# Gated branch of a layer kernel: gate units placed one by one between the chunk steps

## The reference, cut to what matters

```python
log_a = jax.nn.log_sigmoid((g_l @ w2 + g_bias)) / GLA_GATE_NORM
cum = jnp.cumsum(log_a.reshape(b, nc, CHUNK, GLA_HEADS, GLA_DK), axis=2)   # CHUNK = 64, nc = 4
q_dec, k_inv, k_to_end = q * jnp.exp(cum), k * jnp.exp(-cum), k * jnp.exp(cum_last - cum)
attn = jnp.where(tril, jnp.einsum('bnihd,bnjhd->bnhij', q_dec, k_inv), 0.0)
o_intra = jnp.einsum('bnhij,bnjhv->bnihv', attn, v)
def step(state, inp):
    q_c, k_c, v_c, d_c = inp
    o_c = jnp.einsum('bihd,bhdv->bihv', q_c, state)
    return state * d_c[..., None] + jnp.einsum('bjhd,bjhv->bhdv', k_c, v_c), o_c
o = rms_norm(o_intra + o_inter) * norm_g
o_gla = (o * silu(z)) @ w_o                       # z: "gz"
merged = sigmoid(gate_a) * o_mla + sigmoid(gate_b) * o_rwkv + sigmoid(gate_c) * o_gla   # gate_c: "gc"
```

## Time and profile before

| | us |
|---|---|
| median of 3 runs | 2073.42 |
| lowest, highest | 2066.02, 2075.84 |
| span of the profiled execution | 2070.8 |
| TensorE busy | 1960.2 |
| VectorE busy | 1314.5 |
| ScalarE busy | 704.8 |
| GpSimd busy | 77.0 |

### The profile page before, as it was taken

One profiled execution on the slowest core, in us unless ns is written; L12 is line 12 of the kernel. 1 busy time (PEld: TensorE's weight loads), 2 busy tenths in 40 slices (PEclk: granted clock), 3 DMA queues, 4 the chain that ended last, 5 costly groups with the idle time before them and its releaser, 6 DMA issues.

```text
span 2070.8 us, 41540 instructions
## 1 busy us (share of the span) xinstructions
PE 1960.2 (95%) x18039; PEld 1806.4 (87%) x18039; DVE 1314.5 (63%) x1710; ACT 704.8 (34%) x1011; POOL 77.0 (4%) x123
## 2 busy tenths in 40 slices
PE   8998999999799999999998999898999998999898
PEld 8887999998599999989877889897988887889887
DVE  8895388747647866854765358566764576339555
ACT  5562233434623332130423132233231334122233
POOL 2000000000400000020000000000001000000000
PEclk9999999999999999999999999999999999999989
DMA  8544377853437794636430246354654540235433
GB/s 220 141 126 153 120 249 258 269 139 112 121 120 258 241 260 101 171 95 170 115 93 14 76 115 179 82 153 113 174 143 115 140 123 4 63 103 172 113 107 108
DMA packets 473063, 291.41 MB, mean 141 GB/s; under 512 B 26679, under 2 KB 467484, under 8 KB 472776
## 3 DMA queue, kind: packets, MB, share of 16 engines
q1 hardware_dynamic: 466688, 262.20, 45.1%
q0 software_dynamic: 5312, 25.32, 3.2%
q10 hardware_dynamic: 904, 1.58, 0.3%
HBM read 288.02 MB, written 1.05 MB: 140 GB/s over the span
## 4 chain that ended last, share of the span: by engine, by line
PE 82%; DVE 12%; ACT 3%; issue 2%; DMA 1%; POOL 0%; DVEq 0%; ACTq 0%; SPq 0%
PE bank L702 40%; PE bank L1412 6%; PE bank L1414 6%; PE bank L1413 6%; PE bank L691 4%; PE bank L661 2%; PE bank L891 2%; DVE rounded L727 2%; PE bank L883 2%; PE bank L784 1%; PE bank L1599 1%; PE bank L1612 1%; PE bank L1057 1%; PE bank L1580 1%; PE bank L1464 1%
## 5 line engine op out<-in xcount | busy, mean ns | idle before, releaser
L702 PE MATMUL bank<-rounded 128*128 128x256 f32 (+1 forms) x4440 | 540.7, 283 | 10.0 <-DVE rounded L727 7.5
L702 PEld LDWEIGHTS bank<-rounded 128*128 128x128 f32 (+1 forms) x4440 | 531.0, 189 | 16.5 <-DVE rounded L727 10.1
L727 DVE TENSOR_TENSOR rounded<-arena,rounded 128x1024 fp32r<-128x1024 f32 (+1 forms) x243 | 293.2, 1213 | 87.2 <-ACT rounded L716 69.1
L1412 PE MATMUL bank<-parts 128*128 128x256 f32 x1024 | 290.5, 284 | 2.4 <-DVE parts L2164 2.4
L1413 PE MATMUL bank<-parts 128*128 128x256 f32 x1024 | 289.8, 283 | 0.0
L1414 PE MATMUL bank<-parts 128*128 128x256 f32 x1024 | 289.7, 283 | 0.0
L702 PE MATMUL bank<-common,arena 128*128 128x256 f32 x1280 | 285.2, 380 | 0.0
L702 PEld LDWEIGHTS bank<-common,arena 128*128 128x128 f32 x1280 | 240.1, 189 | 39.6 <-issue 4.8
L767 ACT ACTIVATE arena<-bank 128x512 f32<-128x512 f32 x114 | 67.8, 598 | 440.5 <-PE bank L702 427.9
L1412 PEld LDWEIGHTS bank<-parts 128*128 128x128 f32 x1024 | 196.5, 192 | 3.2 <-DVE parts L2164 2.1
L1413 PEld LDWEIGHTS bank<-parts 128*128 128x128 f32 x1024 | 196.5, 192 | 0.1
(11 more groups left out here) (389 smaller groups left out, 2509.3 us busy)
## 6 DMA issues: line engine op xcount, KB each, us to landing
arena<-in_w_in SPq DMA_DIRECT2D x190, 512.0 KB, 3.8
whole<-in_ffn_w_gate_up SPq DMA_DIRECT2D x44, 1024.0 KB, 5.2
arena<-in_ada_w POOLq DMA_DIRECT2D x32, 768.0 KB, 6.5
whole<-in_ffn_w_down SPq DMA_DIRECT2D x16, 1408.0 KB, 7.2
arena<-in_rec_w_in SPq DMA_DIRECT2D x36, 512.0 KB, 3.8
arena<-in_att_w_qkv SPq DMA_DIRECT2D x24, 512.0 KB, 3.7
arena<-in_rec_w_out SPq DMA_DIRECT2D x16, 512.0 KB, 3.5
arena<-in_mla_w_o SPq DMA_DIRECT2D x16, 512.0 KB, 3.7
```

The source lines that it names most:

```text
L702: last = pe.matmul(psum[s][0:c, m % 2 * T:m % 2 * T + T], w[a][:, k, cols], x[b][:, k, :], start=(k, a, b) == (0, 0, 0), stop=k == job.kt ...
L727: dve.tensor_tensor(raw_view(job_of[u], u, UNIT_LOW), raw, high_view(job_of[u], u).bitcast(F32), ALU.subtract)\
L1412: pe.matmul(bank, w_hi, x_hi, start=start and k == 0, stop=False)
```

## The change

The loop over tiles in `gla_pe` is taken apart into five functions, and the calls are put in a new order:

| TensorE, before | TensorE, after |
|---|---|
| gv, gz 0 to 7 | gv, gz 0 to 3 |
| turn 0, scores 0 | turn 0, scores 0, scores 1 |
| chunk states 0, 1 | gz 4, state 0, turn 1, gz 5, state 1 |
| heads of tile 0 | gz 6, heads of tile 0 |
| turn 1, scores 1, state 2 | state 2, gz 7 |
| heads of tile 1 | heads of tile 1 |
| sums, gc 0 to 7, go | gc 0, gc 1, sums, gc 2 to 7, go |

VectorE and ScalarE follow this order. VectorE now makes the low part of gz 7 behind both scores, that of gc 0 ahead of state 1, that of gc 1 ahead of state 2, and that of gc 2 behind the squares. ScalarE takes gz 0 to 3, copies the keys of both tiles, takes gz 4 and 5, makes the high parts of gc 0 and 1, takes gz 6 and 7, and only then loads the table of logarithms. The keys and scores of the second tile have buffers of their own, which lie on GY and GC.

```diff
--- before
+++ after
         G2 = buf(512)
-        KTT = [buf(4, P) for _ in range(2)]
-        AT = buf(4, P)
+        KTT = [[buf(4, P) for _ in range(2)], [flat(GY)[:, c * 512:c * 512 + 512].rearrange("p (a b) -> p a b", a=4) for c in range(2)]]
+        AT = [buf(4, P), flat(GC)[:, 0:512].rearrange("p (a b) -> p a b", a=4)]
         GS = [None] + [buf(4, T) for _ in range(3)]
...
@@ -1797,28 +1797,32 @@
 
         def gla_pe(j):
             pe.wait_ge(layer_split.sem, layer_split.due(pe))
-            for n in ("gv", "gz"):
-                multiply_units(j[n])
+            multiply_units(j["gv"])
+            multiply_units(j["gz"], range(4))
             pe.wait_ge(taken[0].sem, halves(0, j["gv"]))
             pe.wait_ge(taken[1].sem, halves(1, j["gv"]))
             pe.wait_ge(gla_operands.sem, gla_operands.due(pe))
-            for t in range(TT):
+
+            def turn_keys(t):
+                turn_pe([KTE[:, h, t * P:t * P + P] for h in range(4)], abanks)
+
...
+
+            def chunk_state(t, c):
+                for h in range(0, 4, 2):
+                    bank, free, done = vbanks.fill()
+                    pe.wait_ge(free.sem, free.due(pe))
+                    for n in range(2):
+                        last = pe.matmul(bank[:, n * T:n * T + T], KTT[t][c][:, h + n, :], GV[:, t, (h + n) * T:(h + n) * T + T], start=True, stop=True)
+                    last.then_inc(done, 1)
...
                         hh, v = h + n // 2, n % 2
                         o = bank[:, n * P:n * P + P]
-                        last = pe.matmul(o, GV[:, t, hh * T + v * P:hh * T + v * P + P], AT[:, hh, :], start=True, stop=False)
+                        last = pe.matmul(o, GV[:, t, hh * T + v * P:hh * T + v * P + P], AT[t][:, hh, :], start=True, stop=False)
                         for c in range(2):
                             g = 2 * t + c
                             if g:
...
                     last.then_inc(done, 1)
+
+            turn_keys(0)
+            inner_scores(0)
+            inner_scores(1)
+            multiply_units(j["gz"], range(4, 5))
+            pe.wait_ge(token_major.sem, token_major.due(pe))
+            chunk_state(0, 0)
+            turn_keys(1)
+            multiply_units(j["gz"], range(5, 6))
+            chunk_state(0, 1)
+            multiply_units(j["gz"], range(6, 7))
+            heads_of_tile(0)
+            pe.wait_ge(token_major.sem, token_major.due(pe))
+            chunk_state(1, 0)
+            multiply_units(j["gz"], range(7, 8))
+            heads_of_tile(1)
+            multiply_units(j["gc"], range(2))
             sums_pe(SQG, 2, 4)
-            multiply_units(j["gc"])
+            multiply_units(j["gc"], range(2, 8))
             multiply_units(j["go"], pieces=(branch_ready, 1))
 
         @block.tensor
...
             dve.tensor_tensor(KTE, GK, GD, ALU.mult)\
                .then_inc(gla_operands.sem, 1)
             dve.wait_ge(gla_operands.sem, gla_operands.due(dve))
-            split_v(j["gz"].through())
+            split_v(j["gz"].first + 6)
...
+            inner_scores(0)
+            inner_scores(1)
+            split_v(j["gz"].through())
+            next_state(0)
+            split_v(j["gc"].first)
+            next_state(1)
+            dve.nop().then_inc(gla_states.sem, 1)
+            heads_of_tile(0)
+            split_v(j["gc"].first + 1)
+            next_state(2)
+            dve.nop().then_inc(gla_states.sem, 1)
+            heads_of_tile(1)
             squares_v(OG, SQG, DK)
+            split_v(j["gc"].first + 2)
             dve.wait_ge(taken[0].sem, halves(0, j["gz"]))
             dve.wait_ge(taken[1].sem, halves(1, j["gz"]))
             dve.tensor_tensor(OG, OG, GZ, ALU.mult)\
@@ -3412,17 +3442,20 @@
             act.wait_ge(gla_exps.sem, gla_exps.due(act))
             high_act(j["ro"].through())
             take_units(act, j["gv"], keep_tokens(GV))
-            take_units(act, j["gz"], keep(GZ, ACT.Silu))
-            logarithms_act()
+            take_units(act, j["gz"], keep(GZ, ACT.Silu), only=range(2))
             for t in range(TT):
                 bank, full, free = abanks.empty()
                 act.wait_ge(full.sem, full.due(act))
                 for c in range(2):
                     sig = free if c else scalar_step
-                    act.activation(flat(KTT[c]), bank, ACT.Copy, scale=half[:, c:c + 1])\
+                    act.activation(flat(KTT[t][c]), bank, ACT.Copy, scale=half[:, c:c + 1])\
                        .then_inc(sig.sem, 1)
                     act.wait_ge(sig.sem, sig.due(act))
                 act.nop().then_inc(token_major.sem, 1)
+            take_units(act, j["gz"], keep(GZ, ACT.Silu), only=range(2, 3))
+            high_act(j["gc"].first + 1)
+            take_units(act, j["gz"], keep(GZ, ACT.Silu), only=range(3, 4))
+            logarithms_act()
             high_act(j["gc"].first + 2)
             rms_act(256, 4)
             take_units(act, j["gc"], keep(GT, ACT.Sigmoid), high_before(j["gc"], 2))
```

More of the change, by code:

```diff
@@ L1804, in gla_pe, with inner_scores @@
             pe.wait_ge(gla_operands.sem, gla_operands.due(pe))
-            for t in range(TT):
+            def turn_keys(t):
+                turn_pe([KTE[:, h, t * P:t * P + P] for h in range(4)], abanks)
+            def inner_scores(t):
                 here = slice(t * P, t * P + P)
-                turn_pe([KTE[:, h, here] for h in range(4)], abanks)
                 bank, free, done = vbanks.fill()
@@ L1812, in gla_pe, with heads_of_tile @@
                 last.then_inc(done, 1)
[L1813 to L1821, removed]
+            def chunk_state(t, c):
[5 more added lines that the diff above has]
+                    last.then_inc(done, 1)
+            def heads_of_tile(t):
                 pe.wait_ge(gla_states.sem, gla_states.due(pe))
@@ L2872, in gla_v, with inner_scores @@
             dve.wait_ge(gla_operands.sem, gla_operands.due(dve))
-            split_v(j["gz"].through())
+            split_v(j["gz"].first + 6)
             dve.wait_ge(taken[0].sem, halves(0, j["gv"]))
             dve.wait_ge(taken[1].sem, halves(1, j["gv"]))
-            for t in range(TT):
-                here = slice(t * P, t * P + P)
+            def inner_scores(t):
                 bank, full, free = vbanks.empty()
                 dve.wait_ge(full.sem, full.due(dve))
-                dve.tensor_tensor(AT, bank.rearrange("p (a b) -> p a b", a=4), over(const("upto"), 4,
-                    P), ALU.mult)\
+                dve.tensor_tensor(AT[t], bank.rearrange("p (a b) -> p a b", a=4), over(const("upto"), 4, P), ALU.mult)\
@@ L2882, in gla_v @@
                    .then_inc(free.sem, 1)
                 dve.wait_ge(free.sem, free.due(dve))
[L2884 to L2903, removed]
@@ L2904, in gla_v, with next_state @@
-                dve.nop().then_inc(gla_states.sem, 1)
-                if t == TT - 1:
-                    split_v(j["gc"].first + 1)
+            def next_state(g):
+                for h in range(0, 4, 2):
+                    bank, full, free = vbanks.empty()
+                    dve.wait_ge(full.sem, full.due(dve))
+                    for n in range(2):
+                        b = bank[:, n * T:n * T + T]
+                        sig = free if n else vector_step
+                        if g == 0:
+                            dve.tensor_copy(GS[1][:, h + n, :], b)\
+                               .then_inc(sig.sem, 1)
+                        else:
+                            dve.scalar_tensor_tensor(GS[g + 1][:, h + n, :], GS[g][:, h + n, :],
+                                EL[:, (h + n) * 4 + g:(h + n) * 4 + g + 1], b, ALU.mult, ALU.add)\
+                               .then_inc(sig.sem, 1)
+                        dve.wait_ge(sig.sem, sig.due(dve))
@@ L2907, in gla_v, with heads_of_tile @@
+            def heads_of_tile(t):
+                here = slice(t * P, t * P + P)
                 for h in range(0, 4, 2):
```

## The result

| | before | after |
|---|---|---|
| median of 6 runs, us | 2073.48 | 2055.52 |
| lowest to highest, us | 2066.02 to 2080.30 | 2052.68 to 2060.13 |
| span of the profiled execution, us | 2070.8 | 2053.9 |

The ratio of after to before is 0.9913, interval 0.9894 to 0.9931: the changed kernel is 18.0 us, or 0.9%, faster. Two later measurements of the same pair gave 0.9901 (0.9874 to 0.9927) and 0.9891 (0.9861 to 0.992). The forecast was 2057.0 in 2050 to 2068.5. The run of the profiled execution took 2055.73 us, so 1.8 us lie around its span.

A forecast was written before the change was run, and what follows sets the result against it. The prediction took the order of TensorE's queue as the bound. Waits gave 10.8 us and the clock 5.6, together 16.4 off 2073.4: 2057.0 us, range 2050 to 2068.5.

The forecast's parts named there:

- Work that stays: TensorE's pure small steps in one layer's gated branch, start to start without waits: 20.39 us, nothing added or dropped.
- The wait that stays: Before the heads of tile 0, TensorE still waits 0.4 us of 1.50, as gc0's low part precedes state 1.
- Waits that go: Waits for keys (2.12, 0.65 us), state 2 and squares in the gated branch were to be covered or removed.
- The new wait: Inside gc, before its fourth unit, TensorE waits 1.58 us; gc's later end gives back 2.54 us a layer.
- S+4.46: Start of gc's fourth unit, 4.46 us behind S, the end of the sums; it was wanted at S+2.88.
- The 3.30 us wait: Behind gc, TensorE stands 3.30 us until the output weights' first low parts are made; forecast to stay.
- Sum of the waits: Gated branch and gc: waits of 8.18 + 0.17 us become 0.4 + 2.54, gaining 5.4 a layer, 10.8 in both.
- Clock: Second layer's branch lost 7.31 us to low clock; 5.6 us expected back, with 0 and 7.3 as ends.
- (1): Only the waits count; the new order doesn't alter the clock's losses: 2062.6 us, chance 0.22.
- (2): The clock loss moves into gc, where new waits come, 5.7 us back: 2068.3 us, chance 0.16.
- (3): Slower: the small steps spread among units run at 1.2 GHz in both layers: 2096 us, chance 0.04.
- (4): ScalarE high part, VectorE low part, state chain paces TensorE; waits move and don't shrink: 2070 us, chance 0.08.

The follow-up runs named there:

- experiment 4: Changed kernel with one unit of gc ahead of the sums, and VectorE's low parts of gc0 and the first two output units moved: 2038.27 us, ratio 0.9839.
- Experiment 2: Changed kernel with the four gate units put ahead of all chunk steps again, the rest kept: 2081.44 us, ratio 1.0039 to the kernel before.
- Experiments 1 and 3: 1: kernel before with its five waits a branch filled, 2068.78 us; 3: changed kernel with no or one gc unit ahead of the sums, 2054.56 and 2050.16 us.
- filled kernel: Kernel before, own order, with filler matmuls in front of the five waits of each gated branch: 2068.78, 2067.55 and 2068.10 us in three timings.

## Why the prediction was right

- **Work that stays, 20.39 us a layer.** Right. From the first turn to the heads of tile 0 the sum gives 15.24 us with the wait of 0.4 in it; it is 1315.18 - 1299.94 = 15.24. From the first turn to the end of the sums it gives 20.39 + 6 x 2.88 + 0.39 = 38.06; it is 37.88. Switching between steps and units costs nothing in sum.
- **The wait that stays, 0.4 us.** Its cause was right: it is released by VectorE's states behind the low part of gc0, and in experiment 4 it went when that low part was moved. Behind the end of unit 5 (1310.06) the heads start at +5.12, forecast +5.05. That the row's 0.37 equals the forecast is in part luck: the forecast counts from start to start, and counted so, unit 6 and the wait take 1315.18 - 1311.59 = 3.59 us, 0.71 more than the 2.88 of a unit, while state 1 ahead of them took 1.53 where 1.78 was put. In experiment 4 the move was worth 0.64 us.
- **Waits that go.** None stands before states, scores, second heads or sums. Experiment 2 shows that the units between the steps cover the waits for the states: without them 4.33 and 2.33 us appear. For the keys the prediction named unit 4, unit 5 and the table load; experiment 2 shows that the units weren't needed for those.
- **The new wait.** S+4.46 was forecast for the fourth unit; it started at 1342.31, S+4.49. Counted from start to start that is a wait of 1.61 us, forecast 1.58; the row has 1.28, since the modelled end of the matmul before overlaps by some 0.3. The 120 matmuls from there take 15.61 us against 14.6 at full pace, so 1.0 us in small waits where 0.96 was forecast. Experiments 1 and 3 show its cause from the other side: with eight or seven units behind the sums it isn't there.
- **The 3.30 us wait.** Unchanged, as forecast; experiment 4 shows it could have been taken too.
- **Sum of the waits.** 10.8 forecast, 10.96 in the trace, 11.5 between filled and changed kernel.
- **Clock.** The step was the weakest one: 5.6 us taken from one branch of one execution, with 1.7 us of it left as a dip. That the loss goes with the waits was right, and the six traces that keep the covers show no dip in any branch, so the 1.7 us had no counterpart. Filling the waits gave 3.3, 4.6 and 8.8 us, so the size fell among them, but by luck: 7.3 less a dip that did not come happened to lie near 5.3, the mean of three executions. The third trace of before would have said zero, the second 8.7.
- **Rivals.** (1), waits only, 2062.6: excluded by the intervals of the changed kernel's ratios and by the second and third timing of the filled kernel. (2), a loss inside gc: no, gc's units ran at granted clock 1.00 behind the 1.28 us wait in both layers (15.61 and 15.60 us for the 120 matmuls). (3) and (4): not seen in the changed kernel, though experiment 2 shows what (4) looks like when TensorE has nothing to put beside VectorE's chain.

By the Trainium skill, "TensorE: Matmul & The Clock Gate", section "What's actually happening", the mechanism behind the clock is run-variable. The three traces of the kernel before agree: 0 and 7.31, 7.31 and 1.41, 0 and 0 us.

## What to carry to other kernels

When the bounding engine waits at small steps for two others, first reorder the steps themselves (both scores and the second turn earlier, the table load later: 2.8 us of waits a layer here); then count its free-standing units and place them one by one, each behind the step that starts the others' work; then follow the others' queues as well, because a unit moved ahead (here the second of gc) is missed behind. Look for operations that stand behind a wait they don't need: the low parts of go cost 3.3 us a layer that way. Estimate the clock's share from several traces, or measure it by filling the waits with idle matmuls.

## What the runs showed of the hardware that was not expected

- Filler matmuls whose results are thrown away made the kernel faster by 4.6 and 8.8 us in two measurements (and by 3.3 in a third, whose interval reaches 1.0005), though no real instruction of the branch came sooner than in its undisturbed form (28.57 us both).
- A wait's price in clock can come near the wait: in the trace of experiment 2, 12.6 us more of waits went with 10.2 us lost by the clock, at granted clocks of 0.91 and 0.83 over its branches.
- Behind the unchanged 3.30 us wait the same 48 matmuls took 5.90 us in the changed kernel's first layer and 8.53 in its second. Over all twelve traces with that wait they took 5.9 us five times and 7.2 to 8.7 nineteen times, so a fall there is likely but not certain; without the wait (experiment 4) they took 5.82 both times.
